# The order of two waits in the queue of weight loads of a two-layer decoder step

## The chip, the cores and the metric

One core of one Trainium2 chip. The metric is the device time of one execution of the program, in microseconds (us). Several executions were timed; the median is compared.

## The reference

Two layers of a decoder trunk, run for 512 prompt tokens and for 64 sample tokens (8 sequences of 8), D_MODEL = 1024, all in float32. Each layer normalises its rows, multiplies them with `w_in`, runs a gated mixer over chunks of 128 tokens in one half of the width and a differential attention over four heads in the other (the sample tokens also over a paged cache), and adds the product with `w_out` to the rows. Then comes the mixture of experts, on which the change bears:

```python
h = rmsnorm(x, g2).reshape(b * t, d)
pg = softmax(h @ r_g);  gi, gw = argmax(pg), max(pg)       # 1 of 4 groups
le_sel = (h @ r_e) of the group gi                         # 4 experts
tw, ti = top_k(softmax(le_sel), 2);  tw = tw / sum(tw)     # 2 of 4 experts
a = silu(h @ w_gate[e]) * (h @ w_up[e]) * gates[e]         # 16 experts, 1024 -> 256
y = x + sum over e of a @ w_down[e]                        # 256 -> 1024
```

Outputs are the rows of both groups, the new keys and values and one normalised intermediate.

## The kernel before, in words

The program is written out for each engine by hand; each engine runs its own list of instructions in order, and semaphores (`Count`, line 99) tie the lists together. Tokens lie in five tiles of 128 rows, tile 4 being the 64 sample rows.

**Weights** come in pieces of 1 MB (128 partitions of 2048 floats). A layer has 14 dense pieces (`N_DENSE`; ten of `w_in`, four of `w_out`) and 48 pieces of experts, three for each: part 0 and part 1 hold gate and up for the two halves of the contraction, part 2 holds the down projection. They go into ten buffers: six of `ring`, and four others (`others`, line 273) in tiles that the attention no longer needs, `kc`, `vc`, `v` and `kva`. `STEADY` (line 407) says which buffer the first ten expert pieces use, `(6, 4, 7, 5, 0, 2, 8, 3, 1, 9)`; buffers 0 to 5 are the ring, 6 to 9 the others. All pieces are issued by SyncE in one loop (lines 472 to 509), one `dma_start` at line 508 for each. Ahead of each stands a wait on `piece_used` (line 475), which says that the buffer's last reader is done, and a few waits for single pieces (lines 486 to 499).

**Expert slots.** The tokens of the experts, sorted by the size of the experts, fill twelve slots of 128 rows (`SLOTS`, line 89). The first three slots, 0 to 2, take one expert each; later ones share a slot between two or more. `LOADS` (line 397) is the order of the pieces: slot 0 parts 0 and 1, slot 1 part 0, slot 1 part 1, slot 0 part 2, slot 2 parts 0 and 1, slot 1 part 2, and so on. So the fourth piece, `i == N_DENSE + 3`, is part 1 of slot 1 (buffer 5), and the fifth, `N_DENSE + 4`, is part 2 of slot 0 (buffer 0).

**A slot** runs like this. GpSimd gathers its 128 rows from the DRAM tensor `h_rows` by an indirect DMA; TensorE turns them (`turn_in`), multiplies them with parts 0 and 1 (`up`), turns the activated product (`turn_act`) and multiplies it with part 2 (`down`); GpSimd scatters the result. TensorE works on slot n's `up` and slot n - 1's `down` in one pass of its loop (lines 1260 to 1285).

**The first slot is special.** ScalarE stores each tile of normalised rows to `h_rows` as soon as it is ready (`store_rows`, line 1310, semaphores `h_stored` and, for the last tile, `h_last`). The first slot's gather (`gather_first`, line 641) doesn't wait for the last tile, tile 3: it fetches what the other four tiles hold, out of `h_rows` into the tile `ws`, and signals `hs_in[0]`; rows that belong to tile 3 are left out. TensorE turns the fetched rows (`first_turn`, line 1105, waiting for `hs_in[0]`) and adds tile 3's rows by a matmul with a one-hot matrix (`first_late`, line 1113). Behind these in TensorE's list come `up` of slot 0, with `index_rows(1)` inside it, from whose result VectorE works out the rows of slot 1's gather (`index`, line 2041). That gather waits for `h_last` and signals `hs_in[1]`.

**Waits of single pieces on SyncE.** The first expert piece waits for the end of the attention and for the stored keys and values. The fourth (line 494) waits for `hs_in[0]`, the fifth (line 496) for `h_last`, the seventh (line 498) for `hs_in[1]`. All ten buffers are free before the slots begin, apart from these waits; later pieces wait for `piece_used`.

All pieces travel on SyncE's DMA queue (q1 in the profile), the gathers and scatters on GpSimd's (q0), the stores of rows on ScalarE's (q10).

Of the kernel before, what the change touches and what calls it, by code (L numbers as in the profile page):

```python
# [47 lines left out]
N_DENSE = N_IN + N_OUT  # L48
# [98 lines left out]
def layers():  # L147
    for l in range(L):
        Count.layer = l
        yield l  # L150
# [25 lines left out]
def extras(eng, n_extra, slot, done=None, otherwise=None, start=None, **moved):  # L176


    def pair(key, number, q):
        slot(key, 0, number, q)  # L180
        only_if(eng, n_extra > number + 1, lambda: slot(key, 1, number + 1, q), **moved)

    def others():
        with turns(eng, "extra") as q:
            only_if(eng, n_extra > q * 2 + 2, lambda: pair("x", q * 2 + 2, q), **moved)

    def first():
        if start:
            start()
        pair("e", 0, 0)  # L190
        only_if(eng, n_extra > 2, others, **moved)
        if done:
            done()

    only_if(eng, n_extra > 0, first, otherwise=otherwise, **moved)
# [15 lines left out]
def program(nc, totals, d):  # L211
    Count.loops, Count.every, Count.layer = [], [], 0
    with ExitStack() as ctx:
# [3 lines left out]
        def count(name, start=0, answers=None):  # L217
            return Count(ctx.enter_context(nc.semaphore(name)), name, totals, start, answers)
# [48 lines left out]
        hs = hT_cols[:, 0:2 * D].rearrange("p (b n) -> p b n", b=2)  # L267
# [70 lines left out]
        hs_in = [count(f"hs_in{b}") for b in range(2)]  # L338
# [32 lines left out]
        def shares(n):  # L371

            return [(slice(P - sum(w for _, _, w in SLOTS[n][i:]), P - sum(w for _, _, w in SLOTS[n][i + 1:])), pos, first)
                    for i, (pos, first, _) in enumerate(SLOTS[n])]

        def columns(n):

            out, w = [], math.gcd(*(w for _, _, w in SLOTS[n]))
            for at, pos, _ in shares(n):
                begin = at.start  # L380
                while begin < at.stop:
                    out.append((slice(begin, begin + w), pos))
                    begin += w
            return out
# [29 lines left out]
        def piece(i):  # L414
            return ring[:, SLOT[i], :] if SLOT[i] < RING else others[SLOT[i] - RING]

        def freed_before(i):

            earlier = [j for j in range(i) if SLOT[j] == SLOT[i]]
            if i >= N_DENSE and earlier and earlier[-1] >= N_DENSE:  # L420
                return N_DENSE + (i - N_DENSE - BUFFERS) + 1
            if earlier:
                return earlier[-1] + 1
            last = max(j for j in range(PER_LAYER) if SLOT[j] == SLOT[i])
            return (N_DENSE + GONE.index(LOADS[last - N_DENSE]) if last < W_LAYER else last) + 1 - PER_LAYER
# [27 lines left out]
        def extra_slots(eng, name):  # L453

            eng.wait_ge(*dve_s.at("flags"))
            eng.sem_inc(passed[name], 1)
            return eng.value_load(flags[0:1, 0:1], min_val=0, max_val=EXTRA)


        @block.sync  # L460
        def _(sp):

            for c in [*read.values(), piece_used, kc_used, vc_used, x_ready, *hs_used]:
                sp.sem_inc(c.sem, c.begin)
            def x_load(t):
                n = NROW if t == TP else P
                sp.dma_start(x[0:n, t, :], d["xs"] if t == TP else d["xp"][t * P:(t + 1) * P, :]).then_inc(*x_in[t].inc(by=16))

            x_load(0)
            for l in layers():  # L470
                expert_at = {}
                for i in range(W_LAYER):

                    if l * PER_LAYER + freed_before(i) + CREDIT > 0:
                        sp.wait_ge(piece_used.sem, l * PER_LAYER + (freed_before(i) + CREDIT))
                    if i == 2 and l == 0:
                        for t in range(1, NT):
                            x_load(t)
                        sp.dma_start(c32[:, P:NC32], d["c32"][:, P:NC32]).then_inc(*c32_in.inc(by=16))
                        sp.dma_start(cat_cols[:, 0:NC16], d["c16"]).then_inc(*c16_in.inc(by=16))  # L480
                    elif i == 2:

                        Count.layer = l - 1
                        sp.wait_ge(*high_in[TP].at("high"))
                        Count.layer = l
                    if i == N_DENSE:

                        sp.wait_ge(*full["O"].at("o", TP - 1))
                        sp.wait_ge(*full[SO_AT[3]].at("so", 3))
                    if i == N_DENSE + FIRST_OTHER:  # L490

                        sp.wait_ge(*k_stored.at("k"))
                        sp.wait_ge(*v_stored.at("v"))
                    if i == N_DENSE + 3:
                        sp.wait_ge(*hs_in[0].at("hs", "m", 0))
                    if i == N_DENSE + 4:
                        sp.wait_ge(*h_last.at("h"))
                    if i == N_DENSE + 6:
                        sp.wait_ge(*hs_in[1].at("hs", "m", 1))
                    at = l * W_ROWS + i  # L500
                    if i >= N_DENSE:
                        pos, part = LOADS[i - N_DENSE]
                        if pos not in expert_at:
                            if not expert_at:
                                sp.wait_ge(*dve_s.at("order"))
                            expert_at[pos] = sp.value_load(order[0:1, pos:pos + 1], min_val=0, max_val=E - 1)
                        at = expert_at[pos] * PER_EXPERT + (l * W_ROWS + N_DENSE + part)
                    sp.dma_start(piece(i), d["w"][bass.DynSlice(at, 1), :, :].rearrange("a p n -> (a p) n")
                                 ).then_inc(*landed[SLOT[i]].inc("w", i, by=16))
                n_extra = extra_slots(sp, "sp")  # L510

                def load(key, b, number, q):
                    e = sp.value_load(flags[0:1, bass.DynSlice(number + 1, 1)] if key == "x" else flags[0:1, number + 1:number + 2], min_val=0, max_val=E - 1)
                    for j in range(PER_EXPERT):
                        i = EXTRA_AT[key] + b * PER_EXPERT + j
                        sp.wait_ge(piece_used.sem, l * PER_LAYER + q * (2 * PER_EXPERT) + (max(i - RING + 1, W_LAYER) + CREDIT))
                        sp.dma_start(piece(i),
                                     d["w"][bass.DynSlice(l * W_ROWS + e * PER_EXPERT + (N_DENSE + j), 1), :, :].rearrange("a p n -> (a p) n")
                                     ).then_inc(*landed[SLOT[i]].inc("w", i, by=16))

                extras(sp, n_extra, load, arrivals=landed)

            for t in range(NT):
                n = NROW if t == TP else P
                sp.wait_ge(x_ready.sem, L * NT + t + 1)
                sp.dma_start(d["ys"] if t == TP else d["yp"][t * P:(t + 1) * P, :], x[0:n, t, :]).then_inc(*stored.inc(by=16))
            sp.wait_ge(stored.sem, stored.now())
            sp.wait_ge(*v_stored.at("v"))
            sp.wait_ge(*va_stored.at("va"))
            sp.wait_ge(*k_stored.at("k"))  # L530
# [1872 lines left out]
```

## Time and profile before

| | |
|---|---|
| median of 3 runs | 936.6 us (935.08 to 937.87) |
| the profiled execution | 937.48 us, its span 935.7 us |
| TensorE matmul busy | 894.7 us, 96% of the span |
| VectorE busy | 400.9 us, 43% |
| ScalarE busy | 242.6 us, 26% |
| GpSimd busy | 185.8 us, 20% |
| DMA traffic | 197.48 MB, 211 GB/s over the span |
| SyncE's queue q1 (weights) | 136.04 MB, 36.2% of the 16 DMA engines' span |

All times in the trace are us from the start of the span. The trace shows each instruction with its start and its duration, the idle time of its engine ahead of it and what ended that, and for DMAs the packets of each queue and the time from issue to landing. The chain of waits is followed back from the last instruction: at each step to what released it. A time that an engine off this chain loses costs nothing.

### The profile page before, as it was taken

To read this page: it belongs to the slowest core of one execution; us is meant where nothing else is said; L and a number is where in the kernel's file an instruction comes from. 1 tells how busy PE (TensorE), PEld (TensorE's weight loads), DVE (VectorE), ACT (ScalarE), POOL (GpSimd) and SP (SyncE) were. 2 spreads that over 40 slices of the span, in tenths; PEclk is the share of its full clock that TensorE was granted. 3 is DMA by queue.
4 is the path that set the end of the run, shared out by engine and by line. 5 is a ranking of instruction groups with operands and counts; after the bars stand their busy time and mean duration, and the time that the engine had idled before them with its cause. 6 is when DMAs were issued, how large, how long until landed. Compare 5 with 4: busy or idle time off the path is not lost.

```text
span 935.7 us, 13401 instructions
## 1 busy us (share of the span) xinstructions
PE 894.7 (96%) x4836; PEld 432.5 (46%) x4836; DVE 400.9 (43%) x1039; ACT 242.6 (26%) x495; POOL 185.8 (20%) x259
## 2 busy tenths in 40 slices
PE   9999999999999999989799999999999999999991
PEld 6444355556546544333444344455564464433330
DVE  2403225577538646111163032357764575741123
ACT  3211256643102021111131113566420111211110
POOL 2243201331101111110035042013312011111100
PEclk9999999999999999999999999999999999999996
DMA  9716004351015999999583060043410179999996
GB/s 344 288 56 258 23 1 134 97 173 55 2 45 210 339 413 410 420 418 379 219 321 116 4 278 1 0 142 103 169 46 23 63 297 360 421 386 420 420 350 240
DMA packets 38619, 197.48 MB, mean 211 GB/s; under 512 B 6520, under 2 KB 6648, under 8 KB 22672
## 3 DMA queue, kind: packets, MB, share of 16 engines
q1 hardware_dynamic: 19456, 136.04, 36.2%
q0 software_dynamic: 14736, 45.72, 14.2%
q10 hardware_dynamic: 4352, 14.76, 4.4%
q8 instruction: 43, 0.70, 0.3%
q14 instruction: 32, 0.26, 0.1%
HBM read 175.16 MB, written 27.79 MB: 217 GB/s over the span
## 4 chain that ended last, share of the span: by engine, by line
PE 86%; DMA 7%; DVE 4%; issue 2%; ACT 2%; ACTq 0%; DVEq 0%; SPq 0%; POOLq 0%; POOL 0%
PE ps L729 78%; PE ps L727 7%; DMA vc<-in_w 4%; DMA cat<-y_rows 1%; DMA hT<-h_rows,igat 1%; PE ps L745 1%; DMA y_rows<-hn,isca 1%; DVE hT L1608 0%; DVE tmp L1686 0%; DVE tmp L1741 0%; DVE hT L2182 0%; ACT L1430 0%; ACT L1384 0%; ACT L1418 0%; ACT ring L1418 0%
## 5 line engine op out<-in xcount | busy, mean ns | idle before, releaser
L729 PE MATMUL ps<-ring,hT 128*128 128x512 f32 (+4 forms) x1200 | 404.2, 583 | 5.9 <-DMA vc<-in_w 2.7
L729 PEld LDWEIGHTS ps<-ring,hT 128*128 128x128 f32 (+2 forms) x1200 | 153.6, 158 | 210.0 <-issue 206.4
L729 PE MATMUL ps<-ring,cat 128*128 128x512 f32 (+3 forms) x496 | 211.0, 598 | 0.0
L729 PEld LDWEIGHTS ps<-ring,cat 128*128 128x128 f32 (+2 forms) x496 | 74.2, 168 | 80.8 <-issue 79.1
L2182 DVE TENSOR_TENSOR hT<-ps,par 128x512 f32<-128x512 f32 x48 | 31.1, 686 | 131.0 <-PE ps L727 126.0
L670 POOL DMA_INDIRECT y_rows<-hn,isca x24 | 24.1, 1004 | 214.9 <-ACT hn L1512 210.5
L549 POOL TENSOR_TENSOR st<-st,half 128x1 f32<-128x1 f32 (+3 forms) x60 | 63.0, 1050 | 11.1 <-POOL st L547 10.7
L1629 DVE TENSOR_REDUCE st<-sqj 128x8 f32<-128x512 f32 x20 | 13.5, 681 | 111.5 <-ACT sqj L1346 111.4
L547 POOL TENSOR_SCALAR st<-st 128x1 f32<-128x1 f32 (+3 forms) x60 | 16.3, 272 | 222.6 <-DVE st L1629 81.7
L729 PE MATMUL ps<-hT,ring 128*128 128x512 f32 x128 | 57.1, 599 | 0.7 <-DVE tmp L1686 0.7
L1512 ACT COPY hn<-ps 128x1024 f32<-128x1024 f32 x22 | 22.3, 1012 | 87.6 <-PE ps L729 81.6
L729 PE MATMUL ps<-kc,hT 128*32 128x512 f32 (+2 forms) x160 | 44.2, 598 | 0.0
L555 POOL DMA_DIRECT2D kc<-in_ck x32 | 24.6, 768 | 96.0 <-PE ps L729 71.7
L1418 ACT ACTIVATE ring<-ps,st 128x128 f32<-128x128 f32 (+3 forms) x64 | 33.2, 524 | 28.8 <-DVE st L1753 28.6
L729 PEld LDWEIGHTS ps<-hT,ring 128*128 128x128 f32 x128 | 23.7, 190 | 29.9 <-issue 28.4
L1346 ACT ACTIVATE sqj<-ps,st 128x512 f32<-128x512 f32 (+1 forms) x20 | 13.7, 686 | 89.0 <-PE ps L729 89.0
L555 POOL DMA_DIRECT2D vc<-in_cv x32 | 17.6, 550 | 87.7 <-PE ps L729 71.5
L662 POOL DMA_INDIRECT hT<-h_rows,igat x22 | 23.3, 1058 | 51.1 <-DVE isca L2052 46.2
L1495 ACT ACTIVATE cat<-ps 128x256 f32<-128x256 f32 x24 | 9.2, 383 | 92.2 <-PE ps L729 92.2
L729 PE MATMUL ps<-vc,hT 128*32 128x512 f32 (+2 forms) x128 | 29.2, 596 | 0.9 <-issue 0.9
L1608 DVE TENSOR_TENSOR hT<-ps,g_sb 128x512 f32<-128x512 f32 x20 | 13.0, 687 | 39.1 <-PE ps L727 39.0
L729 PE MATMUL ps<-v,cat 128*64 128x512 f32 (+1 forms) x96 | 29.2, 597 | 0.0
(295 smaller groups left out, 1080.2 us busy)
## 6 DMA issues: line engine op xcount, KB each, us to landing
ring<-in_w SPq DMA_DIRECT2D x80, 1024.0 KB, 11.3
kc<-in_w SPq DMA_DIRECT2D x12, 1024.0 KB, 15.6
vc<-in_w SPq DMA_DIRECT2D x12, 1024.0 KB, 15.8
v<-in_w SPq DMA_DIRECT2D x10, 1024.0 KB, 14.3
kva<-in_w SPq DMA_DIRECT2D x10, 1024.0 KB, 14.7
kc<-in_ck POOLq DMA_DIRECT2D x32, 256.0 KB, 3.7
vc<-in_cv POOLq DMA_DIRECT2D x32, 256.0 KB, 3.2
h_rows<-qk ACTq DMA_DIRECT2D x10, 512.0 KB, 2.6
```

The lines of the kernel that those rows point to most:

```text
L547: nc.gpsimd.tensor_scalar(stat["ms"][at, 0:n], src, 1.0 / size, EPS, ALU.mult, ALU.add).then_inc(*pool_c.inc())
L549: nc.gpsimd.tensor_tensor(dst, stat["ms"][at, 0:n], half[at, 0:n], ALU.pow).then_inc(*pool_c.inc(*label))
L555: pool.dma_start(buffer(b % 2, g), view(d[table][bass.DynSlice(l * NPOOL + page, 1)])).then_inc(*arrived[b % 2].inc("kv", b, by=16))
L662: pool.indirect_dma_start(hs[:, b, :], None, h_rows, bass.IndirectOffsetOnAxis(index, 0), bounds_check=TOK - 1, oob_is_err=False).then_inc ...
L670: pool.indirect_dma_start(rows, bass.IndirectOffsetOnAxis(index, 0), y_sb[:, b, :], None, bounds_check=rows.shape[0] - 1, oob_is_err=False ...
L727: ins = pe.transpose(out, lhsT, rhs)
L729: ins = pe.matmul(out, lhsT, rhs, start=start, stop=stop, skip_group_check=loose)
L1346: nc.scalar.activation(sqj[at, t % 2, :], bank(u)[at, :], ACT.Square, scale=stat["rs"][at, t:t + 1]).then_inc(*act_s.inc("sq", name, t))
L1418: ins = nc.scalar.activation(e_sb[:, n % 2, m, 0:(i + 1) * P], bank(f"S{n % 2}", m)[:, 0:(i + 1) * P], ACT.Exp, bias=stat["nb"][:, c:c + 1 ...
L1512: nc.scalar.copy(y_sb[:, b, :], ps[:, 6:8, :].rearrange("p a n -> p (a n)")).then_inc(*read["O"].inc("down", *key))
L1629: vec.tensor_reduce(stat["ssk"][:, 8 * t:8 * t + 8], groups(sqj[:, t % 2, :], 8, DK), AX.X, ALU.add).then_inc(*dve_s.inc("ss" + name, t))
L2182: vec.tensor_tensor(hsT[:, b, hf * HALF:(hf + 1) * HALF, :], bank(f"T{hf}").rearrange("p (j t) -> p j t", j=HALF), g, ALU.mult).then_inc(* ...
```

## The change

The wait of the fourth expert piece for the first slot's gather is taken out. The fifth piece, which waited for the last store of rows, waits for that and then for the gather. The loop, the order of the pieces and their buffers stay as they are.

```diff
--- before.py
+++ after.py
@@ -491,10 +491,9 @@
 
                         sp.wait_ge(*k_stored.at("k"))
                         sp.wait_ge(*v_stored.at("v"))
-                    if i == N_DENSE + 3:
-                        sp.wait_ge(*hs_in[0].at("hs", "m", 0))
                     if i == N_DENSE + 4:
                         sp.wait_ge(*h_last.at("h"))
+                        sp.wait_ge(*hs_in[0].at("hs", "m", 0))
                     if i == N_DENSE + 6:
                         sp.wait_ge(*hs_in[1].at("hs", "m", 1))
                     at = l * W_ROWS + i
```

## Rows read from the trace of the kernel before

**Rows 1.** the page's part 4, the chain that ended last, by engine

```profile
PE 86%; DMA 7%; DVE 4%; issue 2%; ACT 2%; ACTq 0%; DVEq 0%; SPq 0%; POOLq 0%; POOL 0%
```

**Rows 2.** the chain in order of time, its two gathers (start, us, what)

```profile
311.40 4.40 DMA hT<-h_rows,igat
...
770.51 4.75 DMA hT<-h_rows,igat
```

**Rows 3.** SyncE's queue in order of time, layer 0 (start, us, instruction)

```profile
293.05 0.34 SPq L508 DMA_DIRECT2D vc<-in_w  x1
303.46 3.52 SPq L508 DMA_DIRECT2D ring<-in_w  x3
316.04 0.33 SPq L508 DMA_DIRECT2D v<-in_w  x1
```

**Rows 4.** SyncE's waits (total us, times, longest us)

```profile
SPq L495 <- DMA ws<-h_rows,ifirst: 20.0, 2, 10.2
SPq L499 <- DMA hT<-h_rows,igat: 17.0, 2, 8.8
SPq L497 <- DMA h_rows<-qk: 3.3, 2, 1.7
```

**Rows 5.** GpSimd in order of time, three of its gathers

```profile
298.89 1.17 POOL L646 DMA_INDIRECT ws<-h_rows,ifirst  x1 [14.38 <-DVE ifirst L2010]
...
327.06 0.99 POOL L662 DMA_INDIRECT hT<-h_rows,igat  x1 [12.23 <-DVE isca L2052]
...
758.72 1.17 POOL L646 DMA_INDIRECT ws<-h_rows,ifirst  x1 [14.36 <-DVE ifirst L2010]
```

**Rows 6.** DMA issues of the whole execution, us to landing

```profile
ws<-h_rows,ifirst POOLq DMA_INDIRECT x2, 4.4
```

**Rows 7.** DMA queues from 298.89 to 300.5 us (packets, MB, share)

```profile
q1 hardware_dynamic: 82, 0.62, 91.4%
```

**Rows 8.** DMA queues and issues from 300.5 to 303 us

```profile
q0 software_dynamic: 144, 0.38, 51.2%
...
q1 hardware_dynamic: 11, 0.01, 1.0%
...
h_rows<-qk ACTq DMA_DIRECT2D x1, 512.0 KB, 2.9
```

**Rows 9.** TensorE's weight loads in order of time, first slot, both layers

```profile
304.06 1.03 PEld L729 LDWEIGHTS ps<-c,ws 128*128 128x128 f32 x8
...
763.24 1.87 PEld L729 LDWEIGHTS ps<-c,ws 128*128 128x128 f32 x16
```

**Rows 10.** TensorE in order of time, its idle before weights, both layers

```profile
415.77 0.61 PE L729 MATMUL ps<-ring,hT 128*64 128x512 f32 x1 [1.67 <-DMA kc<-in_w]
...
421.06 0.61 PE L729 MATMUL ps<-ring,hT 128*64 128x512 f32 x1 [1.26 <-DMA vc<-in_w]
...
874.20 0.61 PE L729 MATMUL ps<-ring,hT 128*64 128x512 f32 x1 [0.63 <-DMA kc<-in_w]
...
879.66 0.61 PE L729 MATMUL ps<-ring,hT 128*64 128x512 f32 x1 [1.44 <-DMA vc<-in_w]
```

**Rows 11.** DMA queues from 327.06 to 331 us

```profile
q1 hardware_dynamic: 228, 1.66, 100.9%
```

**Rows 12.** DMA queues from 331 to 335.5 us

```profile
q1 hardware_dynamic: 201, 1.47, 81.9%
q0 software_dynamic: 143, 0.36, 20.9%
```

**Rows 13.** three stretches (us, busy by engine, granted clock PEclk, DMA share, GB/s)

```profile
core 0: us, PE busy (x) PEld busy (x) DVE busy (x) ACT busy (x) POOL busy (x), PEclk, DMA share, GB/s
301.00:302.00 1.00, 1.00 (x6) 1.00 (x6) 0.61 (x4) 0.72 (x1) 0.25 (x1) 0.50 0.69 209
414.00:415.00 1.00, 0.11 (x4) 0.00 (x0) 0.00 (x0) 0.82 (x1) 0.00 (x0) 1.00 0.99 397
918.00:919.00 1.00, 0.00 (x0) 0.00 (x0) 0.00 (x0) 0.00 (x0) 0.00 (x0) 0.79 0.52 180
```

## What the change will do to the time

> **What bounds the kernel now.** Start with the chain of waits: TensorE is 86% of it and the DMA 7% [rows 1]. So a change to one load pays or costs only where TensorE waits for a DMA. In time order the chain runs, in each layer, through the gather of the second slot's rows (4.40 and 4.75 us) [rows 2]. Right before that stands the stretch this change touches, the hand-over from the output projection to the first expert slot. The layer in the first half of the trace is layer 0, the other layer 1.
>
> SyncE's own queue shows how the weight pieces go out there. Call them p0 to p11, as `i` is `N_DENSE` to `N_DENSE + 11`. p2 goes out at 293.05; nothing follows until 303.46, where p3, p4 and p5 go within 3.5 us; p6 goes at 316.04 [rows 3]. Its waits name the causes: p3 waits up to 10.2 us for the first slot's gather, p4 another 1.7 us for the last store of normalised rows, p6 up to 8.8 us for the second slot's gather [rows 4].
>
> GpSimd starts the first slot's gather at 298.89 and 758.72 [rows 5], and it lands 4.4 us later in both layers [rows 6]. Two windows of the DMA view say how it travels. From 298.89 to 300.5 only weight packets move, with no packet of the gather [rows 7]; from 300.5 to 303 there are 144 gather packets and hardly any weights [rows 8]. So 1.6 us go by to the first packet, and 2.8 us from there. Today the three pieces happen to be drained just when its first packet is ready. In layer 0 it lands at 303.3, and TensorE loads the first of its rows at 304.06: 0.75 us of slack. In layer 1 it lands at 763.12 and TensorE takes it at 763.24: 0.1 us, none to speak of [rows 9].
>
> Further on the weights do bind: TensorE idles 1.67 and 1.26 us for pieces in layer 0, 0.63 and 1.44 in layer 1, together 5.0 us [rows 10]. That is what earlier weights could win.
>
> **The change, part by part.**
> 1. p3's wait goes. Its buffer was last read by the dense pieces of the query stage, and as scratch of the attention, for whose end p0 waits already; so nothing else holds it. It leaves right behind p2, at about 293.4 in place of 303.46 [rows 3]. One DMA moves; SyncE had nothing else to issue in between.
> 2. The three pieces were drained by about 300.5 [rows 7, 8]. A fourth megabyte at the loaded rate of 1.66 MB in 3.94 us [rows 11] adds 2.5 us, so weights now flow until about 303.0, across the whole time in which the gather had the DMA engines to itself.
> 3. What that does to the gather is not in the trace, because no gather of before meets exactly 2.5 us of weights. Its bounds: at best nothing, 4.4 us as now. At worst as the gather issued at 327.06 into a stream that never stops [rows 5]: no packet for 3.94 us [rows 11], and then 143 packets spread over 4.5 us among 201 of weights [rows 12]. That is 8.4 us to its last packet against 4.1 now (298.89 to 303), +4.3 us. I take the loaded start of 4.0 us, since weights keep coming for 4.1 us after the issue, and the unloaded 2.8 us from there, since they end just then: 6.8 us, a landing 2.4 us later in each layer. The nearest row below that is the second slot's gather in layer 1, which set out with weights still flowing and took 4.75 us [rows 2].
> 4. TensorE's queue is in order: behind this wait stand the turning of the slot's rows, then both gate-and-up halves, then the index matmuls for the second gather. Delay beyond the slack passes through. Layer 0: 2.4 - 0.75 = 1.65 us. Layer 1: 2.4 - 0.1 = 2.3 us.
> 5. p4 now waits for the last store and then for the gather. It did wait for both before, since p3's wait stood ahead of it on SyncE. The store (2.9 us from issue to landing [rows 8]) shares its time with the late gather now, so p4 and p5 go out some 0.6 us later. That costs nothing: p6, issued 10 us behind them [rows 3], feeds a later matmul, and the first wait for weights of that stage is at 415.77 [rows 10].
> 6. With p3 gone from the 303-to-313 stretch, p5 lands earlier, and the second gather meets no weights. In layer 1 it may fall from 4.75 to the 4.40 of layer 0 [rows 2], a gain of 0.35 us; in layer 0, none.
> 7. Does the weight stream run ahead by the megabyte? p6 and all later pieces start behind the second gather's landing [rows 4], and that comes after the first. p3 used to be in SBUF before p6 left in any case. So the early megabyte only lengthens the lull before 316.04, and those waits [rows 10] stay. They don't absorb the delay either, because TensorE and the pieces it waits for are shifted by the same amount.
>
> The sum: 1.65 + 2.3 - 0.35 = +3.6 us. The profiled execution took 937.48 us (span 935.7), 0.9 over the median of 936.6; to 941.1 for it, and **940.2 us** for the median, 0.38% slower. About 0.3%, 2.8 us, is what a measurement of this kernel can tell from no change.
>
> The Trainium skill, "DMA: Bandwidth & Descriptors", section "Queues, rings and completion order", says that each DMA engine takes turns between the queues that it has work for, packet by packet. By that alone the gather would start as now, and the sum would be that of rival A. The shares agree with turns (143 packets beside 201) [rows 12]; the empty 3.94 us ahead of them [rows 11] do not look like a queue that gets its turn at once.
>
> **The rivals.**
> A. *The gather shares from the start.* First packet after 1.6 us as now, then turns with p3. For it: 143 packets beside 201. Beside weights it needs 4.5 us for what it does in 2.5 alone; in the 2.8 us that p3 then lasts it gets 60% through, the rest takes 1.0 us: the landing is 1.3 us late. Layer 0 pays 0.55, layer 1 1.2, less 0.35: +1.4, **938.0 us**. Against it: the empty start [rows 11].
> B. *The gather goes ahead of p3, and the weights gain.* If at 300.5 the engines take the gather before p3's descriptors, it loses nothing; p4 and p5 follow on an emptier link, the second gather lands 0.35 us sooner or more, and everything behind it with it: 936.2. To be faster by more than 2.8 us the stream would have to start far enough ahead to remove the waits for weights [rows 10], at most 5.0 us: **931.6 us** at the end. It decides as soon as p6's issue comes earlier than 316.04 by more than the gather's delay; against it, p6 waits for a gather that depends on the first slot's rows.
> C. *The clock falls as well.* In the same stretch of layer 0 the granted clock was already 0.50 from 301 on [rows 13], the 1.2 GHz level. A new idle of 1.65 or 2.3 us stands in the middle of it. 414 to 415.77 was idle too and stayed at 1.00, whereas the long wait at the end went down at 918 [rows 10, 13]. A fall of about 3 us, as in layer 0, over work that fills TensorE costs half of that, 1.5 us; one or two of them: **941.7 to 943.2 us**.
> That p3 does not move at all would need its buffer to be taken, which part 1 excludes.
>
> **How the numbers follow.** Forecast, the gather late by about 2 to 3 us: 0.45. Rival C on top of it: 0.13. A: 0.34. B: 0.08, of which 0.06 beyond 0.3%. The forecast's lower edge (a landing 2 us late) gives +2.8, the bound, so I count most of it and all of C as slower: 0.55. A, B's small end and a shaved forecast are within 0.3%: 0.39. Faster: 0.06. Range: from B's small end, 936.2, to C with most of two falls, 942.8.
>
> **What would show it.** Right: p3 issued at 293 to 294; no gather packet before about 302.5 and a landing of 6 to 7 us in place of 4.4; TensorE idle before the first slot's rows near 304 and 763; second gather and p6 shifted by 1.5 to 2.5 us; the waits near 415 and 421 as long as before. Wrong: gather packets from 300.5 on beside weights (A); the landing still 4.4 us and p6 earlier than 316.04, with shorter waits near 415 (B); granted clock 0.50 after 305 or after 765 (C).

## The result, and the profile after

The changed kernel takes 943.62 us (941.61 to 945.37, 6 runs) beside 935.84 us for the kernel before in the same runs: a ratio of 1.0063, interval 1.0037 to 1.009, so 5.9 us slower (3.5 to 8.4); the two medians are 7.8 us apart. The profiled execution's span grew from 935.7 to 942.0 us. All lines of code behind the diff are one lower (the matmuls of L729 are now L728).

The page's part 4, the chain by engine, answers to [rows 1]; below it the chain in order of time answers to [rows 2]:

```profile
PE 83%; DMA 10%; DVE 3%; issue 2%; ACT 2%; ACTq 0%; DVEq 0%; SPq 0%; POOLq 0%; POOL 0%
```

```profile
298.52 6.53 DMA ws<-h_rows,ifirst
...
314.95 4.32 DMA hT<-h_rows,igat
...
762.88 5.64 DMA ws<-h_rows,ifirst
```

TensorE's share fell from 86 to 83% and the DMA's rose from 7 to 10%. The first slot's gather, which was not on the chain before, is now on it in both layers. It took 4.4 us [rows 6]; now it takes 6.53 us in layer 0 and 5.64 in layer 1, together 1.3% of the span. Most of the rest of the rise is weight pieces (3.6% before, 6.3% now), through which the chain now runs at other places; what TensorE waited for them stands at the end of this section.

SyncE's queue (start, duration, instruction) and its waits (total us, times, longest) answer to [rows 3, 4]:

```profile
292.69 0.34 SPq L507 DMA_DIRECT2D vc<-in_w  x1
293.22 14.72 SPq L507 DMA_DIRECT2D ring<-in_w  x3
319.48 0.33 SPq L507 DMA_DIRECT2D v<-in_w  x1
```

```profile
SPq L496 <- DMA h_rows<-qk: 24.8, 2, 12.7
...
SPq L498 <- DMA hT<-h_rows,igat: 20.0, 2, 11.3
```

p3 leaves at 293.22, right behind p2. The row merges it with p4 and p5, which wait as before; their first wait is now called after the last store, up to 12.7 us, because that store lands after the gather. p6 leaves at 319.48; against the first gather's issue that is 20.96 us, where it was 17.15 (316.04 - 298.89).

The DMA queues (packets, MB, share of 16 engines) from the gather's issue to 302 us, and in the 2.5 us from there, answer to [rows 7, 8]:

```profile
q1 hardware_dynamic: 192, 1.44, 98.8%
```

```profile
q0 software_dynamic: 139, 0.38, 37.6%
q10 hardware_dynamic: 95, 0.37, 35.9%
q1 hardware_dynamic: 44, 0.23, 22.0%
...
h_rows<-qk ACTq DMA_DIRECT2D x1, 512.0 KB, 4.2
```

For 3.5 us the weights fill the link and no packet of the gather moves; its first comes between 3.8 and 3.9 us after its issue. Then it goes beside the last store (q10), which takes 4.2 us in place of 2.9. Layer 1 is alike: in the 3.6 us from its gather's issue (762.88 to 766.48) no packet of the gather moves either, and its first comes within the next 0.2 us:

```profile
q1 hardware_dynamic: 205, 1.55, 101.6%
```

From there layer 1's gather has less to do: its 144 packets carry 0.26 MB, where layer 0's carry 0.38.

TensorE's instructions at the first slot, in the kernel before and then in the changed one (start, duration, what; in brackets the idle time ahead of it), and the granted clock by stretch (PEclk, third from the right), against [rows 9, 13]:

```profile
304.23 1.95 PE L729 MATMUL ps<-c,ws 128*128 128x128 f32 x16
306.02 1.95 PE L729 MATMUL ps<-oS,qk 128*128 128x128 f32 x16
```

```profile
305.09 3.78 PE L728 MATMUL ps<-c,ws 128*128 128x128 f32 x16 [1.39 <-DMA ws<-h_rows,ifirst]
308.66 3.11 PE L728 MATMUL ps<-oS,qk 128*128 128x128 f32 x16
...
768.56 2.05 PE L728 MATMUL ps<-c,ws 128*128 128x128 f32 x16 [0.30 <-DMA ws<-h_rows,ifirst]
```

```profile
core 0: us, PE busy (x) PEld busy (x) DVE busy (x) ACT busy (x) POOL busy (x), PEclk, DMA share, GB/s
304.00:305.00 1.00, 0.00 (x0) 0.00 (x0) 0.05 (x1) 0.00 (x0) 0.00 (x0) 0.50 0.70 287
310.00:311.00 1.00, 1.00 (x6) 1.00 (x6) 0.32 (x1) 0.00 (x0) 0.00 (x0) 0.50 0.86 336
311.00:312.00 1.00, 1.00 (x8) 0.81 (x7) 0.90 (x5) 0.00 (x0) 0.00 (x0) 0.95 0.95 352
766.00:767.00 1.00, 1.00 (x7) 1.00 (x7) 0.86 (x5) 0.61 (x2) 0.00 (x0) 0.50 0.85 340
```

TensorE idles 1.39 us for the gather in layer 0 and 0.30 us in layer 1. In layer 0 it then turns the rows in 3.78 and 3.11 us, which took 1.95 and 1.95: the granted clock is 0.50, the 1.2 GHz level, until about 311. It had fallen at 301, ahead of the wait, as in the kernel before [rows 13]; there it was nearly back by 305:

```profile
304.00:305.00 1.00, 1.00 (x9) 1.00 (x9) 0.76 (x5) 0.10 (x1) 0.00 (x0) 0.91 1.39 361
```

So in layer 0 more was lost than the wait; whether the wait kept the clock down, this pair of profiles can't say. In layer 1 the clock was low before the wait too (0.50 in 766 to 767), so TensorE came late to the gather and waited only 0.30 us.

Last, the waits for weights, against [rows 10]:

```profile
397.76 0.63 PE L728 MATMUL ps<-kc,hT 128*32 128x512 f32 x3 [0.33 <-DMA ring<-in_w]
...
420.03 0.81 PE L728 MATMUL ps<-ring,hT 128*64 128x512 f32 x1 [2.07 <-DMA kc<-in_w]
...
858.64 0.63 PE L728 MATMUL ps<-kc,hT 128*32 128x512 f32 x3 [0.39 <-DMA ring<-in_w]
...
880.54 0.61 PE L728 MATMUL ps<-ring,hT 128*64 128x512 f32 x1 [1.70 <-DMA kc<-in_w]
...
885.84 0.61 PE L728 MATMUL ps<-ring,hT 128*64 128x512 f32 x1 [1.28 <-DMA vc<-in_w]
```

They are still there, as forecast: 2.40 us in layer 0 (2.93 before) and 3.37 in layer 1 (2.07 before), together 5.8 us where they were 5.0. Layer 0's 2.07 us of idle was followed by a fall of the clock that cost its next matmuls another 1.7 us (16 of them in 5.35 us to 3.65 in layer 1).

### The profile page after: what moved, and what is told of

It reads as the page before. It is cut to its first block, busy times and chain, and to the rows that moved or that the text cites. A ratio compares the mean times of both kernels' runs of the same rounds, so it can differ in the third digit from the quotient of the medians.

```text
span 942.0 us, 13399 instructions
## 1 busy us (share of the span) xinstructions
PE 899.1 (95%) x4836; PEld 435.4 (46%) x4836; DVE 400.9 (43%) x1039; ACT 242.8 (26%) x495; POOL 187.1 (20%) x259
## 4 chain that ended last, share of the span: by engine, by line
PE 83%; DMA 10%; DVE 3%; issue 2%; ACT 2%; ACTq 0%; DVEq 0%; SPq 0%; POOLq 0%; POOL 0%
PE ps L728 76%; PE ps L726 7%; DMA ring<-in_w 3%; DMA kc<-in_w 2%; DMA vc<-in_w 2%; DMA ws<-h_rows,ifirst 1%; DMA cat<-y_rows 1%; DMA y_rows<-hn,isca 1%; PE ps L744 0%; DMA hT<-h_rows,igat 0%; DVE tmp L1685 0%; DVE tmp L1740 0%; ACT L1429 0%; ACT L1383 0%; ACT L1417 0%
## 5 line engine op out<-in xcount | busy, mean ns | idle before, releaser
L728 PE MATMUL ps<-ring,hT 128*128 128x512 f32 (+4 forms) x1200 | 405.9, 585 | 6.1 <-DMA kc<-in_w 3.8
L728 PEld LDWEIGHTS ps<-ring,hT 128*128 128x128 f32 (+2 forms) x1200 | 153.9, 158 | 211.6 <-issue 208.1
L728 PE MATMUL ps<-ring,cat 128*128 128x512 f32 (+3 forms) x496 | 211.0, 598 | 0.0
L728 PEld LDWEIGHTS ps<-ring,cat 128*128 128x128 f32 (+2 forms) x496 | 74.1, 167 | 80.8 <-issue 79.2
L1628 DVE TENSOR_REDUCE st<-sqj 128x8 f32<-128x512 f32 x20 | 13.5, 681 | 111.5 <-ACT sqj L1345 111.4
L728 PE MATMUL ps<-hT,ring 128*128 128x512 f32 x128 | 57.1, 599 | 0.7 <-DVE tmp L1685 0.7
L728 PE MATMUL ps<-kc,hT 128*32 128x512 f32 (+2 forms) x160 | 45.8, 609 | 0.7 <-DMA ring<-in_w 0.7
L728 PEld LDWEIGHTS ps<-hT,ring 128*128 128x128 f32 x128 | 23.7, 190 | 29.9 <-issue 28.4
L728 PE MATMUL ps<-vc,hT 128*32 128x512 f32 (+2 forms) x128 | 29.2, 596 | 0.9 <-issue 0.9
L728 PE MATMUL ps<-v,cat 128*64 128x512 f32 (+1 forms) x96 | 29.1, 597 | 0.0
## 6 DMA issues: line engine op xcount, KB each, us to landing
ring<-in_w SPq DMA_DIRECT2D x80, 1024.0 KB, 12.7
```

The lines of the kernel that those rows point to most:

```text
L728: ins = pe.matmul(out, lhsT, rhs, start=start, stop=stop, skip_group_check=loose)
L1628: vec.tensor_reduce(stat["ssk"][:, 8 * t:8 * t + 8], groups(sqj[:, t % 2, :], 8, DK), AX.X, ALU.add).then_inc(*dve_s.inc("ss" + name, t))
```

## The experiments

p3 is the fourth piece of experts, `N_DENSE + 3`. The short diffs are against the changed kernel, or against the kernel before where that is said.

**The change without the moved wait.**

```diff
                     if i == N_DENSE + 4:
                         sp.wait_ge(*h_last.at("h"))
-                        sp.wait_ge(*hs_in[0].at("hs", "m", 0))
```

> The changed kernel without its second half: p3 is free, p4 waits for the last store alone. Theory (the whole cost is p3's megabyte in the way of the first gather; the moved wait costs nothing): as the changed kernel, some 6 us over the kernel before (4 to 8). Rival (p4 and p5, held longer by the added wait, make the later weights late): 2 us or more below the changed kernel, and shorter waits for weights near 415 and 875. In the trace p4 should leave at about 306 as in the changed kernel, because the last store lands after the gather.

Measured: 942.37 us, ratio 1.0065 (1.0035 to 1.0095). The gather took 6.56 and 5.89 us. So the second half of the change costs nothing that an interval of 0.3% either way would show; the loss comes from p3's early start. As p4 waits for a store that lands after the gather, the added wait never decides, and this run serves below as another sample of the changed kernel.

**Three pieces free.**

```diff
-                    if i == N_DENSE + 4:
-                        sp.wait_ge(*h_last.at("h"))
-                        sp.wait_ge(*hs_in[0].at("hs", "m", 0))
```

> The suspected cost tripled: p3, p4 and p5 all leave without a wait for the gather or the last store, so weights flow until about 308. Theory: no packet of the gather for about 4 us, then turns with weights; it lands 8 to 10 us after its issue in place of 6.5 and 5.6 in the changed kernel, TensorE waits 3 us or more longer in each layer, and the kernel is 10 to 15 us slower than before. Rival (only the megabyte right ahead of the gather counts, for example because the engines take up to one piece at a time): the same 6 us as the changed kernel.

Measured: 951.09 us, ratio 1.0144 (1.0116 to 1.0172), 13.5 us slower than before. The chain and TensorE's first rows (idle in brackets):

```profile
300.62 9.39 DMA ws<-h_rows,ifirst
...
765.57 9.26 DMA ws<-h_rows,ifirst
```

```profile
310.05 3.79 PE L725 MATMUL ps<-c,ws 128*128 128x128 f32 x16 [4.67 <-DMA ws<-h_rows,ifirst]
...
774.87 3.75 PE L725 MATMUL ps<-c,ws 128*128 128x128 f32 x16 [4.52 <-DMA ws<-h_rows,ifirst]
```

The dose sets the size: 9.39 and 9.26 us for the gather, 4.67 and 4.52 us of idle. The rival that only the megabyte right ahead counts falls. Here both layers turn their rows at half the clock.

The DMA queues show that the delay has two parts. First the 4.3 us from the gather's issue (300.62 to 304.92), then the 5.0 us from there:

```profile
q1 hardware_dynamic: 249, 1.79, 99.5%
```

```profile
q1 hardware_dynamic: 175, 1.29, 68.8%
q0 software_dynamic: 144, 0.38, 20.9%
q10 hardware_dynamic: 55, 0.23, 10.9%
```

No packet of the gather moves for 4.3 us, which is 0.4 to 0.5 us longer than behind one free megabyte. Then it goes, although 1.9 MB of the weights that were queued before it have still to move, and its 144 packets take turns with theirs for 5 us. In layer 1 the first packet comes between 4.2 and 4.3 us, behind 1.81 MB. So here only the first part of the queue holds up the gather's start; the rest slows it by sharing.

**Half of p3 free.**

```diff
+                    if i == N_DENSE + 3:
+                        load_part(i, at, slice(0, PIECE // 2))
+                        held = at
+                        continue
...
                         sp.wait_ge(*hs_in[0].at("hs", "m", 0))
+                        load_part(i - 1, held, slice(PIECE // 2, PIECE), "w", i - 1)
```

`load_part`, not shown, issues the given columns of a piece.

> Half the dose: only half of p3 (every row's first 4 KB) leaves without a wait; its other half goes with p4, behind the last store and the gather. Theory (the gather starts when the weights ahead of it are drained): weights end 1.25 us later than before, the gather lands 5.0 to 5.6 us after its issue, and the kernel is 1.5 to 4 us slower than before. Rival (any weights still queued when the gather is issued cost the full loaded start): 6.5 us and the full 6 us. Rival (half a megabyte hides): within 1 us of before.

Measured: 939.47 us over 10 runs, ratio 1.0023 (1.0006 to 1.004): 2.2 us slower. The chain's row in layer 0, TensorE in both layers, and the gather of layer 1 in the DMA view (us to landing, last):

```profile
298.84 5.33 DMA ws<-h_rows,ifirst
```

```profile
304.22 3.78 PE L737 MATMUL ps<-c,ws 128*128 128x128 f32 x16 [0.25 <-DMA ws<-h_rows,ifirst]
...
765.12 2.11 PE L737 MATMUL ps<-c,ws 128*128 128x128 f32 x16
```

```profile
ws<-h_rows,ifirst POOLq DMA_INDIRECT x1, 4.4
```

In layer 0 the gather lands after 5.33 us, as the theory has it. In layer 1 it lands after 4.4 us, as in the kernel before, so there the theory missed and half a megabyte hides; TensorE starts the rows 5.21 us after the issue (759.91) without having waited. Of the 2.2 us the wait is only 0.25; in layer 0 the rows were turned at half the clock.

The four doses side by side, times in us from the gather's issue, weights as q1 moved them from that issue until it was empty:

| p3 to p5 free | weights still queued, layer 0 | first packet, layer 0 | landing, layers 0 and 1 | kernel slower by |
|---|---|---|---|---|
| none | 0.63 MB | 1.8 to 1.9 | 4.4 and 4.4 | 0 |
| 0.5 MB | 1.1 MB | 2.6 to 2.8 | 5.33 and 4.4 | 2.2 |
| 1 MB | 1.7 MB | 3.8 to 3.9 | 6.53 and 5.64 | 5.9 |
| 3 MB | 3.7 MB | 4.3 to 4.4 | 9.39 and 9.26 | 13.5 |

Up to 1 MB the first packet comes about when the weights ahead of the gather are drained. With 3 MB it comes well before that, and the rest of the delay comes from sharing with the weights that are left.

**p3 in the middle of the gather** (against the kernel before).

```diff
                     if i == N_DENSE + 3:
-                        sp.wait_ge(*hs_in[0].at("hs", "m", 0))
+                        sp.wait_ge(*pool_c.at("rs2", TP - 1))
                     if i == N_DENSE + 4:
                         sp.wait_ge(*h_last.at("h"))
+                        sp.wait_ge(*hs_in[0].at("hs", "m", 0))
```

> p3 is let go neither at 293 nor at the gather's landing, but when GpSimd has finished its first arithmetic behind the gather's issue, at about 301.2 and 761, half a microsecond or more after the gather's first packets. Theory (weights that are ahead of the gather hold up its start): its first packet comes 1.6 us after its issue as before, it lands at most 1 us late, and the kernel takes the time of the kernel before, within 1.5 us. Rival A (all weights beside the gather slow it by taking turns): a landing 1.3 us late or more, some 1 to 3 us slower than before. Rival (a new loss that does not hang on the order at all): 4 us slower or more.

Measured: 948.69 us, ratio 1.0119 (1.0097 to 1.0141), 11 us slower: the third rival's number, though the first part of the theory held. The first slot's rows start on time, and the loss is elsewhere. TensorE, the chain and the DMA queues from 305.5 to 310.5 us:

```profile
303.29 1.95 PE L730 MATMUL ps<-c,ws 128*128 128x128 f32 x16
...
320.55 1.97 PE L728 MATMUL ps<-c,hT 128*128 128x128 f32 x8 [5.83 <-DMA hT<-h_rows,igat]
```

```profile
302.26 8.50 DMA h_rows<-qk
311.81 8.69 DMA hT<-h_rows,igat
```

```profile
q1 hardware_dynamic: 78, 0.51, 32.7%
q10 hardware_dynamic: 144, 0.52, 25.6%
```

The rows are turned at 303.29, 4.60 us after the gather's issue, at full clock. But the store of the last rows, issued at 302.26 behind p3, which left at 301.27, takes 8.50 us in place of 2.9. The second gather waits for that store, and so do p4 and p5, which now go out together with it: it takes 8.69 us in place of 4.4, and TensorE idles 5.83 us (5.80 in layer 1). So the hold that the kernel before has on p3 guards two transfers, the gather and, right behind it, the store. Part of the store's delay is the late start again: from 302.26 to 305.5 p3 moves 0.54 MB and no packet of the store moves. Why the two then move only 1.03 MB in 5 us, no run here shows.

**TensorE kept busy.** Four pairs of idle matmuls in layer 0 and two in layer 1, then seven and one, in place of one:

```diff
-                keep_busy(1)
+                keep_busy(2 if l else 4)
                 first_turn(0)
```

> The changed kernel with more idle matmuls in TensorE's list just before the first slot's rows (4 pairs in layer 0 and 2 in layer 1, in place of 1), whose results nobody reads. Theory with the clock (about half of layer 0's loss is the granted clock of 0.50 that lasts until 311 because TensorE idles from 303.7 to 305.1): granted clock back at 1.00 by about 305, the first slot's rows turned in 1.95 and 1.95 us in place of 3.78 and 3.11, and 2 to 3 us less than the changed kernel. Rival (the clock was low by chance of that stretch, not because of the idle): no gain, or up to 1 us slower.

Measured: 942.25 us, ratio 1.0044 (1.0019 to 1.0068).

```diff
-                keep_busy(1)
+                keep_busy(1 if l else 7)
                 first_turn(0)
```

> The changed kernel with 7 pairs of idle matmuls in place of 1 just before the first slot's rows in layer 0 (layer 1 as it is), so that TensorE is busy until the gather lands. Theory (the idle of TensorE makes layer 0's clock fall or stay low): granted clock back before the first slot's rows, 1.95 us for them, TensorE's wait gone, 1.5 to 3 us less than the changed kernel. Rival (the clock is low there for another reason): rows turned in 3.5 us or more as in four profiles so far, and no gain or a loss of 1 us.

Measured: 942.92 us over 10 runs, ratio 1.0052 (1.0033 to 1.0071). TensorE in layer 0, first with four pairs, then with seven:

```profile
305.02 3.56 PE L728 MATMUL ps<-c,ws 128*128 128x128 f32 x16 [1.19 <-DMA ws<-h_rows,ifirst]
```

```profile
303.74 3.33 PE L744 MATMUL ps<-c 128*128 128x128 f32 x14
306.87 2.29 PE L728 MATMUL ps<-c,ws 128*128 128x128 f32 x16
```

With four pairs it still waits 1.19 us and turns the rows at half the clock. With seven the wait is gone and the rows are turned in 2.29 us, but the filler itself ran at half the clock (14 matmuls in 3.33 us) and put the first rows 7.98 us behind the gather's issue, where they start after 6.6 without it. Both intervals hold the changed kernel's 1.0063: no gain from the filler can be told, and what the clock alone costs is not settled by it.

**Both kernels again**, for the scatter between profiles, twice each; the kernel before first.

> The kernel before, once more, for a second profile of it. Theory (the loss lies at the first slot; what the later stretch adds is scatter between executions): gather of the first slot 4.4 us again, second slot's rows multiplied 18 to 19 us after the first gather's issue; from there to the last scatter's issue the two layers take 139 to 141.5 us, so that stretch differs by 1 us or more from the first profile's 140.2 and 139.2 in one of them. Rival (the later weights are late because of the change): 139.2 to 140.2 again, below the changed kernel's 141.4 and 140.6.

> A third profile of the kernel before. Over its first two, the stretch from the second slot's first gate-and-up matmul to the last scatter's issue took 139.2 to 140.2 us in four layers, and the first slot's rows were turned at half the clock in one of four. Theory (the change costs 0.7 us a layer in that stretch, by weights that arrive later against TensorE): 139.2 to 140.3 again, and no wait for a ring piece ahead of the waits for kc and vc. Rival (that stretch only scatters): 140.5 or more in one of the layers, with such a wait.

> The changed kernel, once more, for a second profile. Theory: gather of the first slot 6.5 us in layer 0 and 5.6 to 5.9 in layer 1 again; layer 0's first rows turned at half the clock again (3.5 us or more in place of 1.95). Rival (half the clock there is chance): 1.95 us.

> A third profile of the changed kernel. Theory (0.7 us a layer in the stretch behind the second slot's first matmul): 140.3 to 141.4 us there in both layers, with a wait of 0.3 to 0.6 us for a ring piece. Rival (scatter): below 139.9 in one layer. In either case the first slot's gather takes 6.5 us in layer 0 and 5.6 to 6.1 in layer 1, and the first rows are turned at half the clock in about every second layer.

Measured: single runs of 939.04 and 935.45 us (before) and 942.39 and 942.30 us (after). The table has the seven profiles of the kernel before, of the changed kernel and of the run without the moved wait; times in us, counted from the issue of the first slot's gather to the first matmul on its rows, from there to the first gate-and-up matmul of slot 1, and from there to the issue of the layer's last scatter. A star marks first rows turned at half the clock (3.47 us or more).

| profile | layer 0 | layer 1 |
|---|---|---|
| before | 5.34, 13.17, 140.20 | 4.62, 13.52, 139.23 |
| before, second | 4.61, 13.08, 139.66 | 5.48, 14.62*, 140.24 |
| before, third | 4.59, 13.03, 140.23 | 4.62, 14.05, 138.43 |
| after | 6.57, 15.78*, 141.35 | 5.68, 13.11, 140.60 |
| after, second | 6.58, 13.16, 140.42 | 6.05, 15.60*, 140.35 |
| after, third | 6.72, 14.90*, 139.90 | 5.54, 13.13, 140.73 |
| after without the moved wait | 6.61, 14.92*, 139.89 | 5.93, 13.18, 141.13 |

Rows that stand behind the stars, from the second profile of before in layer 1 and the second of after in both layers, and one wait for weights of the third of before:

```profile
762.75 3.47 PE L729 MATMUL ps<-c,ws 128*128 128x128 f32 x16
```

```profile
305.24 2.05 PE L728 MATMUL ps<-c,ws 128*128 128x128 f32 x16 [1.82 <-DMA ws<-h_rows,ifirst]
...
765.95 3.78 PE L728 MATMUL ps<-c,ws 128*128 128x128 f32 x16 [1.06 <-DMA ws<-h_rows,ifirst]
```

```profile
393.62 0.63 PE L729 MATMUL ps<-kc,hT 128*32 128x512 f32 x3 [0.70 <-DMA ring<-in_w]
```

The first column separates the kernels in every profile, in layer 1 by as little as 0.06 us (5.48 and 5.54). The second is set mostly by the clock: starred in 4 of 8 layers with p3 free, in 1 of 6 without; in the two starred layers of the first and second profiles of after the rows cost 2.99 and 2.61 us more than 3.9, in the other two 1.8 and 1.7.

All twelve profiles of this document, 24 layers, say more on the clock than the table. In 14 of the layers it was still at 1.00 when TensorE had done what stands ahead of the first rows. Six of these did not wait for the gather, and all six turned the rows at full clock. Eight waited: five turned them at half the clock (waits of 1.19 to 4.67 us), three did not (0.75, 0.94 and 1.82). In the other ten the clock had fallen earlier, two of them in the kernel before, and four turned the rows at half of it. So a fall goes with the wait more often than not, but not always, and it also comes without one.

The third column overlaps: 138.43 to 140.24 before, 139.89 to 141.35 after, 0.88 us apart in the mean (139.67 and 140.55). The wait for a ring piece, which the first pair of profiles shows in after alone, comes in before as well (0.70 us at 393.62) and is missing in the third profile of after. About half of the 0.88 us is TensorE busy for longer: 137.8 us in layer 0 of after and in layer 1 of its third profile, where the clock fell behind a wait for `kc`, beside 136.1 to 136.2 in every other layer. The rest is longer idle. The stretch does not grow with the dose: it took 139.97 and 139.84 us with half of p3 free, 139.48 and 140.53 with three pieces. So the later stretch may add something on average, or only scatter; no run here shows which.

## Why the prediction was right, point by point

The direction was right, and so was the mechanism: the gather's start is held up by the fourth megabyte, and TensorE waits for it. The size was low: +3.6 us forecast, +5.9 measured (3.5 to 8.4). By the ratio, the 936.6 us from which the forecast was counted become 942.5, just inside the range, which ended at 942.8; the changed kernel's own median of 943.62 lies above it. That the sum came as near as it did is partly luck: TensorE's delay was forecast too large, and two terms that it put at nothing, the clock and the later stretch, came on top.

- **The gather (step 3) was the right place.** Forecast: first packet after 4.0 us, landing after 6.8, in both layers. Measured in layer 0: first packet after 3.8 to 3.9 us, landing after 6.53, and 6.54 and 6.68 in the other profiles. In layer 1 the first packet came after 3.6 to 3.8 us and the landing took 5.64, 6.01 and 5.49 us: there 2.8 us from first packet to landing was too much, for a gather of 0.26 MB. The 2.8 us, and the 1.6 us ahead of them, were also read from the edge of a window at 300.5; the first packet of the kernel before comes 1.8 to 1.9 us after the issue in layer 0. The Trainium skill, "DMA: Bandwidth & Descriptors", section "Queues, rings and completion order", has the engines take turns between queues packet by packet. By turns from the start (rival A) the first packet would have come as early as in the kernel before; the empty 3.8 and 3.6 us say otherwise, in both layers. With three pieces free the turns do come, but only behind 4.3 us. The landing alone, 1.2 us late in layer 1, would have looked like rival A.
- **TensorE's delay (step 4).** Forecast 1.65 and 2.3 us, together 3.95. From the table's first numbers: layer 0 from a mean of 4.85 to 6.62, +1.8; layer 1 from 4.91 to 5.80, +0.9; together 2.7. The layer 1 term was mis-sized by the earlier landing and by slack that varies: 5.48 in one profile of before, where the filler matmuls ahead of the rows ran at half the clock and made TensorE late. Layer 0's 0.75 us of slack was such a case too: in the profile from which it was read those ten matmuls took 2.48 us from 301.12 on, in the other two of before 1.36, and there TensorE starts the rows 4.61 and 4.59 us after the issue, with next to no slack.
- **The second gather (step 6).** Forecast: 0.35 us sooner in layer 1, nothing in layer 0. At full clock the second numbers are 13.11 to 13.18 in layer 1, where before had 13.52 and 14.05, and 13.16 in layer 0 beside 13.03 to 13.17. That is as forecast, but the 0.35 us lie within the scatter of before, whose second gather in layer 1 took 4.75, 4.32 and 5.29 us.
- **The clock (rival C) was the term left out of the sum.** The means of the second numbers go from 13.09 to 14.69 in layer 0, +1.6, and from 14.06 to 13.76 in layer 1. I gave the fall of the clock 0.13; it came in half of the layers. That it follows from TensorE's idle is suggested by the counts (none of six layers without a wait, five of eight with one), but the wait of 1.82 us that did not bring it, the layers where the clock had fallen before the wait, and the two fillers keep it from being shown.
- **The later stretch (step 7).** The megabyte gained nothing, as forecast: no weights arrive sooner, since p6 leaves behind the second gather. The forecast put 0 there; the mean difference is +0.88 us a layer, scatter not excluded and cause open.
- **The moved wait (step 5)** costs nothing that shows in the run without it.

The sum of the means is 1.8 + 0.9 + 1.6 - 0.3 + 2 x 0.88 = 5.8 us, beside 5.9 measured and 5.4 between the mean spans of these profiles. Of it the 2.7 us of the gather are shown by the experiments; the clock's part and the later stretch are measured, but their cause is not shown. Rival B falls: p6 left later, and the waits for weights together did not shrink.

## What to carry to other kernels

A small transfer on which the next stage hangs can be late for bulk that was queued before it. Here its start was held up by up to 4.3 us, in which 1.8 MB of weights moved, and what was still queued then shared the engines with it. So look at how much is still queued when it is issued, and let the bulk behind it start only once the small transfer has landed. Free buffers alone are no reason to load early; ask whether the stream behind the early piece can move up too. And before a hold is moved, list every transfer that it guards, the later ones too: here a store stood 3.6 us behind the gather.

## What was not expected

- A load that starts between two small transfers, behind the gather and ahead of the store, can cost more than one ahead of both. With p3 at 301.27 the store took 8.50 us, with p3 at 293 it took 4.2, with p3 behind the gather 2.9.
- The gather did not wait for the whole queue. With 3.7 MB of weights ahead of it, the gather's first packet came after 4.3 to 4.4 us, with 1.9 MB of them still to move.
- The same kernel shows the granted clock of the first slot's rows at 0.50 in some executions and layers and at 1.00 in others (the table's stars), which is worth 1.5 to 3 us each time; single profiles of these kernels can't be compared to better than that.
